# A software pipeline over the head groups of block one in a two-block hybrid network

## The reference: what is computed

```python
z = centred_token_shift(z, mu_prev, mu_next)     # z + mu_prev*(prev - z) + mu_next*(next - z)
r, k, v, lw, la, lg = split(z)
decay = exp(-exp(-softplus(-(w0 + tanh(lw) @ w2)) - 0.5))
iclr = sigmoid(a0 + la @ a2);  gate = sigmoid(lg) @ g2
kk = k * k_k;  kk = kk / max(sqrt(sum(kk*kk)), 1e-12)
for each direction d:                            # forward, and backward in time
    state = state * w_t + (state @ -kk_t) (kk_t * a_t) + v_t k_t ;  y_t = state @ r_t
y = groupnorm(y_forward + y_backward) * gn_g + gn_b
out = (y + sum(r * k * r_k) * v) * gate
```

## Time and profile before

| | us |
|---|---|
| median of 3 runs (4854.64 to 4862.35) | 4862.07 |
| the profiled execution | 4859.53 |
| span of its trace, first to last instruction | 4857.8 |
| PE busy in the span | 4502.2 |
| DVE busy | 1481.6 |
| ACT busy | 828.7 |
| POOL busy | 146.4 |

### The profile page before, as it was taken

How to read it: one execution, slowest core, us unless ns; L and a number is a source line. 1 busy time by engine, 2 the same in 40 slices (tenths; PEclk the granted TensorE clock), 3 DMA queues, 4 the chain that set the end, 5 groups by cost and what they waited for, 6 DMA issues and landing times.

```text
span 4857.8 us, 60662 instructions
## 1 busy us (share of the span) xinstructions
PE 4502.2 (93%) x25140; PEld 2959.1 (61%) x25140; DVE 1481.6 (30%) x3621; ACT 828.7 (17%) x2097; POOL 146.4 (3%) x144
## 2 busy tenths in 40 slices
PE   7888898998999888888998999999999999999999
PEld 3755665443444466567443444477887788788888
DVE  2654662111000456546111000222122322212332
ACT  3112211001000211212101000122222212222220
POOL 0000000000000000000000000000110000001000
PEclk9898898999999988989999999999999999999999
DMA  3010011221222100100221222111111111111111
GB/s 107 15 40 31 10 40 35 87 83 57 74 77 75 56 18 23 39 22 19 76 87 57 74 78 74 56 57 44 53 48 48 53 61 57 48 53 53 53 53 66
DMA packets 71344, 261.62 MB, mean 54 GB/s; under 512 B 7920, under 2 KB 7920, under 8 KB 70816
## 3 DMA queue, kind: packets, MB, share of 16 engines
q1 hardware_dynamic: 69168, 250.62, 14.9%
q10 hardware_dynamic: 1904, 7.11, 0.4%
HBM read 253.51 MB, written 4.19 MB: 53 GB/s over the span
## 4 chain that ended last, share of the span: by engine, by line
PE 89%; DVE 5%; ACT 3%; DVEq 1%; issue 1%; DMA 0%; ACTq 0%; SPq 0%; PEldq 0%
PE ps L2075 27%; PE ps L1313 23%; PE ps L2186 9%; PE ps L1482 4%; PE ps L2152 3%; PE ps L1332 2%; PE ps L1416 2%; PE ps L2105 2%; PE ps L808 2%; PE ps L816 2%; PE ps L823 1%; PE ps L782 1%; PE ps L2086 1%; PE ps L2096 1%; ACT arena L958 1%
## 5 line engine op out<-in xcount | busy, mean ns | idle before, releaser
L2075 PE MATMUL ps<-xT,ring 128*128 128x512 f32 x2656 | 1185.6, 607 | 73.4 <-ACTq L661 47.1
L2075 PEld LDWEIGHTS ps<-xT,ring 128*128 128x128 f32 x2656 | 514.2, 195 | 738.2 <-issue 738.2
L1313 PE MATMUL ps<-xT,ring 128*128 128x264 f32 (+2 forms) x3392 | 795.3, 390 | 17.1 <-DVE arena L1802 10.4
L1313 PEld LDWEIGHTS ps<-xT,ring 128*128 128x128 f32 (+1 forms) x3392 | 640.2, 192 | 135.7 <-DVE arena L1802 13.9
L2186 PE MATMUL ps<-arena,ring 128*128 128x512 f32 x1024 | 440.4, 592 | 1.9 <-issue 1.9
L2186 PEld LDWEIGHTS ps<-arena,ring 128*128 128x128 f32 x1024 | 194.2, 190 | 248.1 <-issue 247.6
L1313 PE MATMUL ps<-arena,ring 128*128 128x264 f32 (+1 forms) x1408 | 320.3, 385 | 2.3 <-DVEq L1702 2.3
L1313 PEld LDWEIGHTS ps<-arena,ring 128*128 128x128 f32 x1408 | 265.9, 191 | 46.3 <-issue 6.1
L1572 ACT ACTIVATE arena<-ps 128x264 f32<-128x264 f32 (+8 forms) x316 | 122.7, 389 | 727.3 <-PE ps L1313 614.1
L958 ACT ACTIVATE arena<-ps 128x128 f32<-128x128 f32 (+1 forms) x296 | 122.8, 424 | 666.7 <-PE ps L2075 330.7
L2096 PE MATMUL ps<-consts,arena 128*128 128x128 f32 x384 | 72.7, 339 | 124.3 <-DVEq L1038 100.7
(11 more groups left out here) (310 smaller groups left out, 4998.4 us busy)
## 6 DMA issues: line engine op xcount, KB each, us to landing
ring<-in_weights SPq DMA_DIRECT2D x467, 512.0 KB, 3.4
arena<-skew_dram ACTq DMA_DIRECT2D x8, 448.0 KB, 3.1
arena<-in_x SPq DMA_DIRECT2D x1, 2048.0 KB, 10.9
out_rows<-arena SPq DMA_DIRECT2D x8, 256.0 KB, 2.7
skew_dram<-arena ACTq DMA_DIRECT2D x4, 511.5 KB, 5.8
consts<-in_const SPq DMA_DIRECT2D x1, 1384.0 KB, 5.9
consts<-in_const ACTq DMA_DIRECT2D x1, 1252.0 KB, 5.6
arena<-in_buckets SPq DMA_DIRECT2D x1, 127.9 KB, 10.9
```

What stands on the lines that cost most here:

```text
L1313: mm = pe.matmul(o[0:m, 0:cols.stop - cols.start], ws[:, k, 0:m], src[:, k, cols], start=k == 0, stop=k == nk - 1)
L2075: m = pe.matmul(o, w[:, k, :], src[:, k, 0:S], start=k == 0, stop=k == KD - 1)
```

## The change

The layer's groups become one pipeline. Instead of one tile list per group there is one per layer, so nothing meets or drains between groups. The next group's zk, zr, zv projections and its w and a products are made in chunk steps 0, 1 and 2 (`FILL`); its decay sums, head norm and scaled keys by DVE and ACT in steps 1 to 3. Projection u stands at the group's head; aq, ak and av stand between the gram products; pool, gate and bsum stand behind the corner products. The last group's norms and its transposes yt and oT are made in the gram and level stages of the next group. POOL gets the token shift of groups 1 to 3 (`shift_z`), the centring and scaling of both norms and the final gating; DVE keeps the sums. ACT gets squares. Sigmoid becomes `0.5 * tanh(x / 2) + 0.5`. ACT's tiles get three PSUM banks and DVE's five. In block two the pair ("A", 1) has its units in another order, and `latent` is made when DVE comes to `vc`, one half at a time. Core of the diff:

```diff
+FILL = [["w0", "w1", "a0", "a1", "zk"], ["zr"], ["zv"], []]
-    ("A", 1): ahead(2) + [("cms",), ("kc",), ("sw", "k"), ("vc",), ("vb",)],
+    ("A", 1): [("kc",), ("sw", "k"), ("cms",), ("vc",)] + ahead(2) + [("vb",)],
...
-        BA, BV = [0, 1], [2, 3, 4, 5, 6, 7]
+        BA, BV = [0, 1, 2], [3, 4, 5, 6, 7]
```

PE, in `group_pe` (the old head, L743 to L768, is gone there):

```diff
+            proj(a, N("u"), ws[c], xT)
+            pe.wait_ge(*at("zshift", it, 2))
+            turn(a, N("vN"), [rkv[:, 2, n * P:(n + 1) * P] for n in range(4)])
             pe.wait_ge(*at("tilde", it, 0))
             turn_keys(0)
             for i in range(2):
                 gram(1, 0, i)
+            proj(a, N("aq"), ws[c], xT)
             pe.wait_ge(*at("tilde", it, 1))
...
+            proj(a, N("ak"), ws[c], xT)
             first_inverse(0)
             gram(2, 0, 0)
+            proj_rows(a, N("av"), ws[c], xT)
...
                 if j < 2:
                     gram(2, 1, j)
+                if j == 3 and c:
+                    tail_pe(pe, L, c - 1, a, turn)
...
+            pe.wait_ge(*at("umix", it))
+            o = a.open(N("pool"))
...
+            o = a.open(N("gate"))
...
+            pe.wait_ge(*at("rkr", it))
+            o = v.open(N("bsum"))
...
+                if c < GROUPS - 1:
+                    if s == 2:
+                        norm_pe(pe, L, c + 1, v)
+                    for n in FILL[s]:
+                        if n == "w0":
+                            rates_pe(pe, L, c + 1, a)
+                        if n[0] == "z":
+                            proj(a, f"{n}@{c + 1}", ws[c + 1], xT)
```

ACT, in chunk step s of `group_act`, behind R:

```diff
+                        if n == "w0":
+                            rates_act(act, L, c + 1, a)
+                        if n[0] == "z":
+                            take_z(act, L, c + 1, a, n)
+                    if s == 1:
+                        keys_act(act, L, c + 1)
                 for d in range(2):
                     take(f"U{d}{s}", Us[d], n=P)
-                take(f"PT{s}", flat(pT))
                 if s < NCH - 1:
                     probs(s + 1)
+                if c < GROUPS - 1:
+                    if s == 2:
+                        load_skew(act, c + 1)
+                        root_act(act, L, c + 1)
+                        exps(act, L, c + 1, 0)
+                take(f"PT{s}", flat(pT))
```

DVE, in chunk step s, ahead of the takes of S:

```diff
+                if s == 2 and c < GROUPS - 1:
+                    norm_bound(dve, L, c + 1, v)
...
+                    if s == 1:
+                        decay_sums(dve, L, c + 1, 0)
+                    if s == 2:
+                        decay_sums(dve, L, c + 1, 1)
+                        norm_keys(dve, L, c + 1)
+                    if s == 3:
+                        keys(dve, L, c + 1)
...
+        def norm_keys(dve, L, c):
+
+            dve.wait_ge(*at("nrm_root", L * GROUPS + c))
+            dve.reciprocal(en[1], en[1])
+            dve.drain()
+            dve.tensor_tensor(kk, kk, en[1], ALU.mult)
```

POOL's new token shift, and block two on DVE:

```diff
+            def shift_z(L, c):
...
+                took(pool, layV, v_pre(L), v_taken, f"bsum@{c - 1}")
+                for j, i in enumerate((1, 0, 2)):
+                    z, dst = zp[:, j % 2, :], rkv[:, i, :]
+                    took(pool, layA, a_pre(L), a_taken, f"{('zk', 'zr', 'zv')[j]}@{c}")
+                    ts(dst, z[:, 1:S + 1], g[:, 56 + i:57 + i], None, ALU.mult)
+                    ts(ztmp, z[:, 0:S], g[:, i:i + 1], None, ALU.mult)
...
+                    tt(dst, dst, ztmp, ALU.add)
...
+                    ts(ztmp, z[:, 2:S + 2], g[:, 3 + i:4 + i], None, ALU.mult)
...
+                    tt(dst, dst, ztmp, ALU.add)
+                    pool.drain().then_inc(STEPS["zshift"][0], 1)
...
-                elif kind == "kc" and hf:
-                    for j in range(2):
-                        latent(L, j)
+                elif kind == "vc":
+                    latent(L, hf)
```

More of the change, by code:

```diff
@@ L316, in build @@
         ra.at = rg.at
-        sig = ra.take(2, S)
-        aa = ra.take(2, S)
+        pr = [ra.take(2, S) for _ in range(2)]
         ra.at = rg.at
-        pr = [ra.take(2, S) for _ in range(2)]
+        win = ra.take(2, S + 16)
+        umix = ra.take(S)
+        ra.at = rg.at + 2 * 2 * S
         rb = Region()
@@ L565, in build @@
         lnV = Tiles(["mean", "var"], BV)
[L566 to L583, removed]
@@ L917, in group_pe @@
                 last = s == NCH - 1
-                o = v.open_all([f"S{d}{s}" for d in range(2) if not last] + [f"Y{d}{s}" for d in range(2)])
+                o = v.open_all([N(f"S{d}{s}") for d in range(2) if not last] + [N(f"Y{d}{s}") for d in range(2)])
                 so, yo = o[:-2], o[-2:]
@@ L961, in flat @@
                 return z.rearrange("p a b -> p (a b)")
-            act.dma_start(skew, skew_dram[bass.ds(c, 1), P - 1:P - 1 + P * (LINE - 1)]
-                          .rearrange("o (p n) -> (o p) n", n=LINE - 1)[:, 0:SKEW]).then_inc(skew_loaded, 16)
-            for i, n in enumerate(("zr", "zk", "zv")):
-                take(n, zp[:, i, 1:S + 1])
-            act.wait_ge(*at("params", it))
-            for t, buf in (("w", sig), ("a", aa)):
-                for d in range(2):
-                    take(f"{t}{d}", buf[:, d, :], ACT.Sigmoid, bias=col(f"{t}0_{d}"))
@@ L1177, in group_dve @@
             gram(2, 0, 1)
-            for d in range(2):
-                for h in range(2):
-                    dve.memset(TT[d][h][half[1 - d], :, half[d]], 0.0)
-                dve.memset(state[d], 0.0)
             dve.drain()
@@ L2132, in _ @@
                     proj(a, f"low{i}", ws, xT)
-                a.end()
+                ws = [Slots(w_grp(L, c)) for c in range(GROUPS)]
+                for c in range(GROUPS):
+                    ws[c].next()
+                proj_z(pe, L, 0, a, ws[0], proj)
+                pe.wait_ge(*at("low_ready", L, 2))
+                rates_pe(pe, L, 0, a)
+                norm_pe(pe, L, 0, v)
+                for c in range(GROUPS):
+                    group_pe(pe, L, c, a, v, ws, proj, proj_rows, turn)
                 flush()
-                for c in range(GROUPS):
-                    group_pe(pe, L, c, proj, proj_rows, slot, free, flush, turn, meet)
+                tail_pe(pe, L, GROUPS - 1, a, turn)
+                a.end(), v.end()
                 meet(m_layer(L, 0))
@@ L2261, in _ @@
                     act.activation(low[:, i, :], low[:, i, :], f).then_inc(STEPS["low_ready"][0], 1)
+                take_z(act, L, 0, a, "zv")
+                rates_act(act, L, 0, a)
+                keys_act(act, L, 0)
+                root_act(act, L, 0)
+                exps(act, L, 0, 0)
+                exps(act, L, 0, 1)
+                for c in range(GROUPS):
+                    group_act(act, L, c, a)
+                squares_o(act)
+                squares_y(act, L, GROUPS - 1)
+                roots_tail(act, L, GROUPS - 1)
+                tail_act(act, L, GROUPS - 1, a)
                 a.end()
-                for c in range(GROUPS):
-                    group_act(act, L, c, meet)
                 meet(m_layer(L, 0))
```

664 lines of the change are left out of this document (390 added, 274 removed).

## The result

The changed kernel takes 4692.7 us (median of 4 runs, 4683.6 to 4694.6) against 4861.3 of the kernel before (4 runs, 4854.6 to 4862.4): ratio 0.9657, 95% interval 0.9646 to 0.9669. The gain is 168.5 us where 149 were forecast.

What follows compares the result with a forecast made beforehand. PE bounds the kernel, with idle holes and low clock within groups; 228 us removed, 93 added and 14 from block two give 149 less than 4859.5, plus 2.5 for the median: 4713 us, range 4650 to 4790.

Steps and rivals of the forecast that it cites:

- Boundaries and gram: Between groups: 70 us of tail, 16 and 10 beside it removed; gram stage: 65 us of waits and 18 of slow running.
- rival B: DVE and POOL block one another over SBUF: up to 96 us back, 4809, a third likelier, 4745; chance 0.20 for 4750 to 4810.
- (a): Step 3: PE waits about 5 us for S of step 2, behind the next keys' norm; 31 us added, bounds 3 and 9 each.
- (b): Step 3, after 5 us of idle: the clock falls; 4 us six times, 24 us added, bounds 0 and 8 each.
- (c): Head of each layer: group 0 has too little to cover DVE and ACT; 10.7 us idle, 4 of low clock, 26 added.
- Corner: Corner products: PE's 2.02 us wait for DVE's copies falls to 1.4 us idle; 5 us removed over eight groups.
- (d): Levels: DVE gets the last group's variance and reciprocals, with five banks instead of six; 12 us added, bounds 0 and 5 each.
- Clock: Low clock removed: boundaries 16 us, gram 18, steps 0 and 1 27 (4.5 of 7.5, six times); 24 and 8 added.
- Block two: PE's 6.43 and 6.79 us gaps ahead of vc and slow vc go: 14 us kept of 16.7, bounds 0 and 17.
- POOL: Token shift takes about 7.7 us, with 6 us spare before the keys in step 1; POOL near 35 us per group.
- A: The holes stay warm: low clock behind step 3's wait and in the steps goes, gain about 203 us, 4659; chance 0.14.
- D: Block two's order moves the hole and does not remove it: 14 us back, 4727; its chance lies inside the forecast's 0.52.

Runs made afterwards that it cites:

- e11: Changed kernel with ten extra POOL instructions (128x512 multiplication into scratch and a drain) ahead of the first shift of each next group: 4775.3 us.
- e1: Changed kernel with VectorE computing the next group's key norms in step 3, behind the normalisation of P, not in step 2 ahead of S: 4685.3 us.
- e5: Changed kernel with ScalarE's root and side 0 exponentials for the next group ahead of zv's copy in step 2, during projection zv: 4631.7 us.
- e12: Changed kernel with 2 PSUM banks for ScalarE's tiles and 6 for VectorE's, as in the kernel before, in place of 3 and 5: 4752.2 us.
- e10: Changed kernel with three extra POOL instructions (128x512 multiplication into scratch and a drain) ahead of the first shift of each next group: 4693.7 us.

## Why the prediction was right, and where not

The forecast of 4713 us was 20 us above the result, and its mechanisms are those that the traces show. By its steps:

- *Boundaries and gram.* The 11.7 us tail is gone six times. The gram stage was to have no wait for VectorE: it has 12 us of them, since `tilde(1)` took 5.5 us for its four operations (284.89 to 290.42) instead of 2.7. Aq's 6.9 us would have covered 6.4; they don't cover 9.1 (281.44 to 290.5). That is rival B in small, in a place that the working of POOL did not look at: it looked at the steps only. Its picture of the later instruction blocked in full is too simple as well: VectorE's took 1.0 to 1.8 us instead of 0.69, and POOL's own, begun first, were stretched too (2.57 instead of 1.56, e11).
- *(a)* forecast 5 us in step 3, found 4.50, with the reciprocal of the next keys just ahead of S; 27 us in all where 31 were booked. That P transposed was "hidden by this" was right, and e1 shows by how much: 2.45 of 4.50 us.
- *(b)* 24 us were booked for the low clock behind that hole; without the hole (e5) PE's busy time in the groups is 30.5 us less.
- *(c)* forecast 10.7 us at each head, found 4.64 + 6.71 = 11.35; 4.64 of it stands ahead of u, at ssq, not behind it.
- *Corner* 1.40 us, as forecast. *Bank waits* gone as forecast, but e12 shows the third bank to be worth 59 us where 17 were booked: the 17 are the waits of the old order, and in the new one ScalarE's queue is late just where a bank is short. *(d)* 0.64 + 0.22 us in the levels, against 2.
- *Clock.* This is the mis-sized term. Idle time in the groups should have fallen by 53 us per layer and fell by 50.5. The terms of the clock (16 + 18 + 27 removed, 24 + 8 added) left 14.5 us per layer; PE's busy time fell by 37.5 and 35.3 (624.8 to 587.3, 618.8 to 583.5). Half of PE's busy time at the low clock is an estimate of its cost, in both layers together:

  | us | PE busy at the low clock, before | after | half the difference | booked |
  |---|---|---|---|---|
  | steps 0 and 1, groups with a successor | 97.3 | 26.7 | 35 | 27 |
  | boundaries, w and a products | 55.3 | 0 | 28 | 16 |
  | gram stage | 46.4 | 0 | 23 | 18 |
  | steps of the last groups | 45.6 | 27.3 | 9 | 0 |
  | step 3, behind the new hole | 0 | 55.0 | -28 | -24 |
  | heads of the layers | 0 | 15.3 | -8 | -8 |

  So "I take 4.5 of 7.5" took too little, the boundaries counted the three projections alone, and the last groups were left out. This makes 60 of the measured 73 us; the other 13 these records don't place.
- *Block two* was to give 14 and gave 4.3; *outside* the groups nothing was booked, and 10.3 us were lost. Most of that is pads: 14 waits of 0.52 us more than before make 7.3 us. Another 1.4 came at the start. These errors (21 us, and 5 of idle time in the groups) and the clock's (44) are of opposite sign; that the total came within 20 is partly luck.
- *POOL.* 6 us of slack were forecast, 6.3 found (226.7 to 232.97), and e10 and e11 bracket it. POOL is busy 37 us per group with a successor ((119.0 - 27.7) / 3 + 27.7 / 4), forecast 35.
- *Rivals.* A (203 us) supposed that hole (a) leaves the clock alone. It does not: with the hole gone, 31 us of slower running went beside its own 27. The other half of A, the low clock of steps 0 and 1, came out mostly as A had it. D's number came true in the kernel before (1 us for the new order), not its mechanism: the hole did not move, 10.8 us of idle time were gone, and the clock took them back.

## What to carry over

Moving work of the next tile into the steps of this one pays as long as each engine's queue has a hole where the work is put, not only PE. For each moved piece look at the engine's idle time just ahead of where it stands: 4.9 us of ScalarE work, done in six groups, cost 61 us in one place and nothing some nine microseconds earlier. Here a wait that shrank without vanishing was no half gain (4.50 to 2.45 us gave 7 us, to zero 61): find a place for the work that delays the takers, as taking the takers ahead of it one by one only moved the wait. And a change of the bank split is a change of every tile list that is padded to it.

## What the runs showed of the hardware

- Low clock behind short holes: PE stood 4.5, 3.7 or 2.45 us in step 3, and 3.4 to 17.1 us at 1.2 GHz went with it each time, in all six places together 64.9, 68.3 and 51.2 us. With no hole at all (e5) step 3 had none in any of the six groups. In these traces the part of the price that is clock lay less in the hole's length than in its being there.
- The same instructions of block two ran with 59.6 to 80.3 us of low clock depending on what had gone before; an edit that took out 10.8 us of idle time measured 1 and 13 us. What decides where the clock falls stays open.
- POOL beside VectorE: operations of VectorE with two inputs in SBUF took 1.0 to 1.8 instead of 0.69 us, and POOL's own multiplications 1.9 to 2.6 instead of 1.56 (e11).
